# A two-layer encoder with mixture of experts: the residual in DRAM during the expert stage, with weighted expert rows added to it by indirect stores

## What is computed

```python
def hierarchical_moe(h, ...):
    ...
    weights = pg[:, None] * top_p                      # two experts for each token
    eid = g[:, None] * EXPERTS_PER_GROUP + top_i       # out of 32
    ...
    xs = x2[slot_tok].reshape(n_blocks, MOE_BLK, d)
    def expert_block(args):
        xb, e = args
        hid = jax.nn.silu(xb @ w_gate[e]) * (xb @ w_up[e])
        return hid @ w_down[e]
    ys = lax.map(expert_block, (xs, block_e)).reshape(cap, d)
    out = jnp.zeros_like(x2).at[slot_tok].add(ys * slot_w[:, None])

def reference(...):
    for i in range(DEPTH):
        hn = rmsnorm(x, norm_mix[i])
        x = x + (windowed_gqa_attention(hn, ...) if i % 2 == 0 else differential_attention(hn, ...))
        x = x + hierarchical_moe(rmsnorm(x, norm_ffn[i]), ...)
    return rmsnorm(x, final_norm)
```

## Time and profile before

| | |
|---|---|
| median of 3 runs | 2630.5 us (2630.07 to 2634.17) |
| the profiled execution | 2631.06 us |
| its span | 2629.4 us |
| mean granted clock of PE | 0.951 |
| busy PE / DVE / ACT / POOL | 2330.4 / 1869.7 / 1552.1 / 282.9 us |
| moved by DMA | 538.48 MB |

### The profile page before, as it was taken

The page is one execution under the profiler, slowest core; times in us unless marked ns, Lnnn a source line. Parts: engine busy times, 40 slices in busy tenths (PEclk is TensorE's granted clock), DMA queues, the critical chain, the costliest instruction groups (busy, mean ns, idle before and its releaser), DMA issues. The chain is left out here.

```text
span 2629.4 us, 34467 instructions
## 1 busy us (share of the span) xinstructions
PE 2330.4 (89%) x11464; PEld 1758.9 (67%) x11464; DVE 1869.7 (71%) x2461; ACT 1552.1 (59%) x2036; POOL 282.9 (11%) x260
## 2 busy tenths in 40 slices
PE   7899989569999999929999999998955999999991
PEld 6666658447777777727777777776844777777671
DVE  5775572668898888858556666556256888888895
ACT  5554460447777777735555565555043778777772
POOL 0000020012121111030000000002001122211102
PEclk9999999779999999959999999999977999999996
DMA  3012020469999999852000000002146999999995
GB/s 121 25 55 96 24 72 32 170 227 397 392 395 399 402 394 395 338 174 89 24 24 24 24 24 24 0 24 72 32 171 206 390 394 401 398 394 393 403 360 212
DMA packets 129501, 538.48 MB, mean 205 GB/s; under 512 B 23232, under 2 KB 52032, under 8 KB 80288
## 3 DMA queue, kind: packets, MB, share of 16 engines
q1 hardware_dynamic: 110496, 470.62, 47.1%
q0 software_dynamic: 18944, 67.12, 7.3%
HBM read 487.50 MB, written 50.20 MB: 204 GB/s over the span
## 5 line engine op out<-in xcount | busy, mean ns | idle before, releaser
L1507 DVE TENSOR_TENSOR m_lo_gate<-m_raw_gate,m_hi_gate 128x2048 fp32r<-128x2048 f32 x132 | 298.9, 2290 | 81.7 <-ACT m_hi_gate L1502 79.8
L1507 DVE TENSOR_TENSOR m_lo_up<-m_raw_up,m_hi_up 128x2048 fp32r<-128x2048 f32 x128 | 292.5, 2285 | 7.1 <-ACT m_hi_up L1502 7.0
L1507 DVE TENSOR_TENSOR m_lo_down<-m_raw_down,m_hi_down 128x2048 fp32r<-128x2048 f32 x124 | 280.2, 2283 | 13.7 <-ACT m_hi_down L1502 13.7
L1502 ACT CAST m_hi_down<-m_raw_down 128x2048 fp32r<-128x2048 f32 x124 | 236.2, 1907 | 90.7 <-DMA m_raw_down<-in_moe_w_down_dram 54.8
L1502 ACT CAST m_hi_gate<-m_raw_gate 128x2048 fp32r<-128x2048 f32 x132 | 247.8, 1908 | 25.6 <-DMA m_raw_gate<-in_moe_w_gate_dram 25.4
L1502 ACT CAST m_hi_up<-m_raw_up 128x2048 fp32r<-128x2048 f32 x128 | 244.4, 1911 | 22.2 <-DMA m_raw_up<-in_moe_w_up_dram 21.2
L1622 PE MATMUL m_G<-m_hi_gate,m_x_hi 128*96 128x512 f32 x512 | 206.1, 402 | 11.4 <-DVE m_x_lo L1732 11.3
L1622 PE MATMUL m_U<-m_hi_up,m_x_hi 128*96 128x512 f32 x512 | 205.2, 401 | 0.0
L1623 PE MATMUL m_G<-m_hi_gate,m_x_lo 128*96 128x512 f32 x512 | 204.6, 400 | 0.0
L1624 PE MATMUL m_G<-m_lo_gate,m_x_hi 128*96 128x512 f32 x512 | 202.5, 395 | 0.0
L1623 PE MATMUL m_U<-m_hi_up,m_x_lo 128*96 128x512 f32 x512 | 201.8, 394 | 0.0
(11 more groups left out here) (380 smaller groups left out, 4907.9 us busy)
## 6 DMA issues: line engine op xcount, KB each, us to landing
m_raw_gate<-in_moe_w_gate_dram SPq DMA_DIRECT2D x128, 1024.0 KB, 11.1
m_raw_up<-in_moe_w_up_dram SPq DMA_DIRECT2D x128, 1024.0 KB, 12.8
m_raw_down<-in_moe_w_down_dram SPq DMA_DIRECT2D x124, 1024.0 KB, 12.0
out_rows<-m_y POOLq DMA_DIRECT2D x64, 384.0 KB, 7.5
a1n_rows<-in_diff_w_qkv_dram SPq DMA_DIRECT2D x21, 512.0 KB, 5.5
out_rows<-a0n_gain SPq DMA_DIRECT2D x1, 8064.0 KB, 37.3
x_res<-in_x_dram SPq DMA_DIRECT2D x4, 1024.0 KB, 9.6
a0n_rows<-in_swa_w_o_dram SPq DMA_DIRECT2D x8, 512.0 KB, 3.3
```

The costliest lines, as they stand in the source:

```text
L1502: act.copy(self.hi[w][:, cut], self.raw[w][:, cut]).then_inc(self.hi_done[w], 1)
L1507: eng.tensor_tensor(self.lo[w][:, cut], self.raw[w][:, cut], self.hi[w][:, cut].bitcast(F32), ALU.subtract)\
```

## The change

x leaves SBUF after a route stage's norm has read it, and comes back with the expert outputs already added.

- In the route stage SP stores each tile of x to the DRAM tensor `x_rows` (1024 by 1024), right behind the store of the same tile's normed rows.
- The table gets as many columns again for the weights: the product on PE is 96 by 110, and `row_hot` is made by three operations of 16 by 55 elements. A slot that no token has gets the row number 2048 or above, and the weight 0 (`share`).
- In the expert stage ACT's copy of Y scales by the slot's share, and POOL's store is an indirect DMA that adds y into the rows of `x_rows` (`compute_op=ALU.add`). Gather and store carry a bound of 1023: rows beyond it are neither read nor written. POOL clears xg once before the first gather.
- `Combined` is gone, with `choice_slot`, `out_rows` and the zeros. Layer 1's attention norm and the final norm use `Loaded` with eight loads of one tile each, layer 0's too.
- Layer 1's attention stage no longer stores x. In the final norm the gain is loaded behind x.

The diff, cut:

```diff
 class Loaded(Resident):
...
-            sp.dma_start(self.t.x[:, 2 * i:2 * i + 2, :], self.x_rows[2 * i * P:2 * (i + 1) * P, :]
-                         .rearrange("(a p) n -> p a n", p=P)).then_inc(loaded, 16)
+            sp.dma_start(self.t.x[:, i, :], self.x_rows[i * P:(i + 1) * P, :]).then_inc(loaded, 16)
-class Combined:
...
# route
-                norm.sync_store(sp)
+                norm.sync_store(sp, lambda tt: sp.dma_start(moe.x_rows[tt * P:(tt + 1) * P, :], t.x[:, tt, :])
+                                .then_inc(x_stored, 16))
...
+                sp.wait_ge(x_stored, 16 * NT)
...
-                own(tt_(row_hot[:, :, :], over_slots(row[:, :], CAP),
-                        count_up[:, :].unsqueeze(1).broadcast_to((P, 2 * NT, CAP)), ALU.is_equal))
-                for c in range(TOP_K):
-                    half = row_hot[:, c * NT:(c + 1) * NT, 0:COLS]
-                    own(tt_(half, half, token[:, :].unsqueeze(2).broadcast_to((P, NT, COLS)), ALU.mult))
+                owned, shared = row_hot[:, :, 0:COLS], row_hot[:, :, COLS:2 * COLS]
+                own(tt_(owned, over_slots(row[:, :], COLS),
+                        count_up[:, 0:COLS].unsqueeze(1).broadcast_to((P, 2 * NT, COLS)), ALU.is_equal))
+                own(tt_(shared, owned, over_slots(weight[:, :, :].rearrange("p c a -> p (c a)"), COLS), ALU.mult))
+                own(tt_(owned, owned, over_slots(token[:, :], COLS), ALU.mult))
...
-                own(dve.tensor_copy(moe.table[:, :], L_ps[0:CAP, 0, 0:COLS]))
+                found = L_ps[0:CAP, 0, 0:COLS]
+                own(ts_(pad_row[:, :], found, 0.0, float(NOWHERE + 1), ALU.is_equal, ALU.mult))
+                own(dve.scalar_tensor_tensor(out=moe.table[:, :], in0=found, scalar=-1.0, in1=pad_row[:, :],
+                                             op0=ALU.add, op1=ALU.add))
+                own(dve.tensor_copy(moe.share[:, :], L_ps[0:CAP, 0, COLS:2 * COLS]))
# experts, POOL
                         pool.indirect_dma_start(out=xg[:, :], out_offset=None, in_=self.hn_rows,
-                                                in_offset=bass.IndirectOffsetOnAxis(pick[:, :], 0)).then_inc(gathered, 16)
+                                                in_offset=bass.IndirectOffsetOnAxis(pick[:, :], 0),
+                                                bounds_check=T - 1, oob_is_err=False).then_inc(gathered, 16)
 
                     def store(b):
+                        wait_count(pool, y_added, 16 * b)
+                        pool.tensor_copy(goal[:, :], self.table[:, b:b + 1] if isinstance(b, int) else self.table[:, bass.ds(b, 1)])\
+                            .then_inc(aimed, 1)
                         pool.wait_ge(y_copied, b + 1)
-                        rows = self.out_rows.rearrange("(r c) n -> r c n", c=CAP)
-                        pool.dma_start(rows[b] if isinstance(b, int) else rows[bass.ds(b, 1)].rearrange("r c n -> (r c) n"),
-                                       y[:, :]).then_inc(y_stored, 16)
-
+                        wait_apart(pool, aimed, b + 1, aim_seen)
+                        pool.indirect_dma_start(out=self.x_rows, out_offset=bass.IndirectOffsetOnAxis(goal[:, :], 0), in_=y[:, :],
+                                                in_offset=None, bounds_check=T - 1, oob_is_err=False,
+                                                compute_op=ALU.add).then_inc(y_added, 16)
+
+                    pool.memset(xg[:, :], 0.0).then_inc(cleared, 1)
+                    pool.wait_ge(cleared, 1)
# experts, ACT
-                        wait_count(act, y_stored, 16 * b)
-                        act.copy(y[:, :].rearrange("q (n m) -> q n m", n=2), Y[0:CAP, :, :]).then_inc(y_copied, 1)
+                        wait_count(act, y_added, 16 * b)
+                        share = self.share[:, b:b + 1] if isinstance(b, int) else self.share[:, bass.ds(b, 1)]
+                        act.activation(y[:, :].rearrange("q (n m) -> q n m", n=2), Y[0:CAP, :, :], ACT.Copy, scale=share)\
+                           .then_inc(y_copied, 1)
```

More of the change, by code:

```diff
@@ L132, in complete, with __init__ @@
         pass
-    def add(self, dve, tt):
-        pass
 class Loaded(Resident):
-    def __init__(self, t, x_rows):
+    def __init__(self, t, name, x_rows):
         self.t, self.x_rows = t, x_rows
-        self.loaded = [t.sem(f"x_loaded_{i}") for i in range(NT // 2)]
+        self.loaded = [t.sem(f"{name}_loaded_{i}") for i in range(NT)]
     def load(self, sp):
         for i, loaded in enumerate(self.loaded):
-            sp.dma_start(self.t.x[:, 2 * i:2 * i + 2, :], self.x_rows[2 * i * P:2 * (i + 1) * P, :]
-                         .rearrange("(a p) n -> p a n", p=P)).then_inc(loaded, 16)
+            sp.dma_start(self.t.x[:, i, :], self.x_rows[i * P:(i + 1) * P, :]).then_inc(loaded, 16)
     def complete(self, eng, tt):
-        eng.wait_ge(self.loaded[tt // 2], 16)
-class Combined:
[L157 to L173, removed]
-        for c in range(TOP_K):
[L175 to L184, removed]
+        eng.wait_ge(self.loaded[tt], 16)
 class Norm:
@@ L237, in sync_store @@
               .then_inc(self.rows_stored[tt % self.bufs], 16)
+            beside(tt)
     def sync_stored(self, sp):
@@ L465, in windowed_attention @@
         TB, O = TO[:, 0:2, :], TO[:, 2:4, :]
-        norm = Norm(t, "a0n", gain, sb, TO, Loaded(t, x_rows))
+        norm = Norm(t, "a0n", gain, sb, TO, Loaded(t, "a0x", x_rows))
         q_parts = sb("a0_q_parts", [P, QH, T], F32R)
@@ L844, in route @@
         stepped = v("stepped", 2 * NT * STEPS)
-        expert, row, slot_of_row = (v(what, 2 * NT) for what in ("expert", "row", "slot_of_row"))
+        expert, row = v("expert", 2 * NT), v("row", 2 * NT)
         owner_cmp, ctl_f = v("owner_cmp", (COLS - EXPERTS) * EXPERTS), v("ctl_f", COLS + 1)
@@ L979, in _ @@
                 own(dve.reciprocal(den[:, :], den[:, :]))
-                own(tt_(t.weight[:, 0, :], pg[:, :], den[:, :], ALU.mult))
-                own(tt_(t.weight[:, 1, :], t.weight[:, 0, :], ex[:, :], ALU.mult))
+                own(tt_(weight[:, 0, :], pg[:, :], den[:, :], ALU.mult))
+                own(tt_(weight[:, 1, :], weight[:, 0, :], ex[:, :], ALU.mult))
                 dve.wait_ge(counted, 1)
@@ L1066, in differential_attention @@
         probs = sb("a1_probs", [P, 2, 2, T], F32)
-        norm = Norm(t, "a1n", gain, sb, TO, Combined(t, "a1", t.dram[1], [probs[:, i // 2, i % 2, :] for i in range(4)]))
+        norm = Norm(t, "a1n", gain, sb, TO, Loaded(t, "a1x", x_rows))
         mix = sb("a1_mix", [P, 4, T], F32)
@@ L1105, in _ @@
                 norm.sync_load(sp)
+                norm.source.load(sp)
+                projections.load(sp, 0)
                 sp.dma_start(lam_b[:, :, :], lam.unsqueeze(0).broadcast_to((P, 4, HEAD))).then_inc(lam_loaded, 16)
                 sp.dma_start(sub_g[:, :], subln.unsqueeze(1), allow_slow_non_contiguous=True).then_inc(lam_loaded, 16)
-                norm.source.complete(sp, 1)
-                projections.load(sp, 0)
-                norm.source.complete(sp, NT - 1)
-                for tt in range(NT):
-                    sp.dma_start(x_rows[tt * P:(tt + 1) * P, :], t.x[:, tt, :]).then_inc(x_stored, 16)
                 projections.sync(sp, HEADS)
@@ L1119, in _ @@
             def _(pool):
-                norm.source.gather(pool)
                 pool.iota(bias[:, :].bitcast(I32), pattern=[[-1, SPAN]], base=T - P, channel_multiplier=1).then_inc(iota_done, 1)
@@ L1431, in _ @@
             def _(sp):
+                source.load(sp)
                 sp.dma_start(gain_b[:, :], gain.broadcast_to((P, D))).then_inc(gain_loaded, 16)
@@ L1437, in _ @@
                 sp.wait_ge(stored, 16 * NT)
-            @block.gpsimd
-            def _(pool):
-                source.gather(pool)
             @block.scalar
@@ L1609, in _ @@
                         store(b)
[L1611 removed]
+                    pool.wait_ge(y_added, 16 * (last + 1))
                 def times(pe, out, left, right, K, N, piece):
```

62 lines of the change are left out of this document (21 added, 41 removed).

## The result

The changed kernel takes 2653.28 us (median of 5 runs, 2647.22 to 2656.51) against 2630.5: 1.0084 times as long, 95% interval 1.0065 to 1.0102. A gain of 27 us was forecast, and a loss of 23 came, outside the stated range. The profiled execution has a span of 2651.5 us, 22.1 more than before.

What follows compares the result with a forecast made beforehand. Expert stages were taken as bound by PE early and DMA late, with PE waiting at the norms outside. Terms -19.0 - 13.8 - 5.2 + 5.0 + 4.0 + 2.0 gave -27.0, so 2604 us; range 2596 to 2650.

Steps and rivals of the forecast that it cites:

- What bounds the kernel: Expert stages: PE paces the first half at 17.64 us a block, DMA the rest, needing some 0.2 us more.
- (1): Layer 1's attention norm: without gathers and adds, 25.2 us to the first projection product, a gain of 19.0 us.
- (2): Final norm: without gathers and adds, 28.8 us instead of 42.6, a gain of 13.8 us.
- Term (3): Expert stages: dropped pads bring a block's DMA time to 17.5 us, so PE paces throughout, gaining 5.2 us.
- Term (4): Expert stages: waiting for y's store to land before the next copy costs 0, 14.0 us being under 17.64.
- Term (5): End of each expert stage: the last store stands alone before the barrier, +2.5 us, twice.
- (6): Route stage's tail: larger table and row_hot, small DVE operations and clearing xg, +2.0 us, twice.
- (7): Route stage's norm: eight more stores of x on SP's queue delay DVE, +1 us, twice.
- Rival C: Expert stages: adds hold the DMA engines, 18.6 us a block and up, slower at 2653 us; chance 0.09.
- pads that the bound does not drop: Expert stages, within Rival C: bounds check fails to drop pads, 18.8 us a block, 2664 us; no separate chance.

Runs made afterwards that it cites:

- e4: Changed kernel with pads added too, each to a spare row of its own in a longer x_rows, gather still dropping them: 2657.86 us, 1.0101 of before.
- e9: Like e5, but the k-th token goes to slot 12 (k mod 8) + k div 8: 2653.79 us, 1.0097 of before.
- e5: Changed kernel with slots dealt out: a block's k-th token goes to slot 6 (k mod 16) + k div 16: 2606.41 us, 0.9915 of before.
- e8: e5 with the final norm's gain loaded ahead of x: 2602.49 us, 0.9896 of before.
- e6: Edits of e4 and e5 together, slots dealt out and pads added, against the changed kernel: 2619.88 us, 0.9967 of before.

## Why the prediction was wrong

- **What bounds the kernel** was read rightly: PE's pace and DMA's lie 0.2 us apart, so the stage goes over to DMA at once when DMA's work grows.
- **Terms (1) and (2), the norms,** held: 25.0 us where 25.2 was forecast, 29.6 where 28.8 was, DVE waiting for the gain (8.97 us).
- **Term (3), the expert stages, failed.** It wrote "64 rows gathered 0.6; 64 rows added, 0.6 for the write and 0.6 more", the mean load of 16 engines, and came to 17.5 us a block where 18.67 was measured. The price of the add was nearly right: 0.6 for the write and 0.6 for the read is 1.2 us a block, the packets took 1.39 (88.8 / 64). By the Trainium skill (Collectives: The Full Stack, "The bandwidth ceiling: the fold count and why AG ≠ RS ≠ AR") the add of a ReduceScatter halves the rate because it reads two sources; the page writes that of a collective's ring, and 0.35 against 0.17 us a row agrees for this DMA. The rule, cited for 17.5 us a block, was right about the row and silent about the engines. What failed is "a third of every gather and store on average": with packed tokens the fullest engine keeps six rows of each (e4 adds 32 rows a block for 0.05 us, e9 and the packets show the groups of six). The fullest engine's sum is 3.30 us in place of before's 2.28, 1.0 more, and 18.67 in place of the late 17.85 is what came, 0.8 more.
- The Trainium skill (DMA: Bandwidth & Descriptors, "Why a DMA increments its semaphore by 16 and not by 1") says that some direct copies that POOL issues use all 16 engines with a sixteenth of the partitions each, rounded up; 96 partitions would give six each, an estimate from that rule. It says so of direct copies; e5 and e9 agree with it for the indirect ones. It was there to be read and was not put to the sum.
- **Term (4), y's round trip at 0,** held: at most 13.1 us to the landing, against a bound of 15.9. **Term (5)** was +2.5 twice, and came as +1.2 and +4.2, so 5.4 for 5.0. **Terms (6) and (7)** were +3.0 a layer; +2.4 and +1.1 came. A profiled execution is too coarse for that check: e5 and e8 have the same instructions up to the final norm, and their first copies of Y start at 590.2 and 585.5 us. The three operations took 1.08 us each, as forecast. PE's table product, priced at +0.8, was shorter than before:

```profile
525.05 1.08 DVE L980 TENSOR_TENSOR m0r_row_hot<-m0r_row,m0r_count_up 128x880 f32<-128x880 f32 x1
...
530.20 4.90 PE L882 MATMUL m0r_L<-m0r_row_hot,m0rn_hnT 128*96 128x110 f32 x32 [16.43 <-DVE m0rn_hnT L984]
```

- **Rival C** had the outcome to the microsecond (2653) with 0.09 of the chance. That is luck in the number: 18.6 us a block was where that rival began and no sum of anything, and its reason, the adds hold the engines, is the add's price, which was nearly right and in the forecast already. It stood beside the case of pads that the bound does not drop, at 2664; in effect that is what happened, with pads that are dropped and save nothing. The range ended 3 us below the result because most of C lay outside it.

What stays open: why the gather's rows weigh more on the interval than their packets' time. From e4 to e6 two rows less on the fullest engine are 0.4 us by the price and 0.8 measured. A gather's packets are spread over as long a time as an add's (3.84 and 3.75 us for 96 rows) though each is shorter (0.21 and 0.34 us); whether that is the reason was not tried. That a slot belongs to an engine in sixes is inferred from e5, e9, the sum and the packets in flight; no record names the engine of a packet.

## What to carry to other kernels

The indirect transfers here, spread over 16 engines, ended with their fullest engine, so price one by the rows of that engine, not by bytes over the total rate; dropped rows paid only when they were dealt over all engines. With the valid rows of an indirect DMA packed at the front, a bound that drops a third of the adds bought 4.6 us here, no more than the noise, with the rows dealt out 13.5, and the dealing alone turned a loss of 0.8% into a gain of 0.85%. An added row cost its DMA engine two plain ones (0.34 and 0.17 us), and that is worth paying where DMA has slack, or where it empties a stage border (32 us at the two norms).

## What was unexpected of the hardware

- DMA share is no measure of a DMA limit here: it is 1.00 in the DMA-paced window of e9 and 0.99 in the PE-paced one of e5, at 364 and 374 GB/s.
- POOL's issue of an indirect DMA depends on what runs beside it. The add's issue took 2.28 us in the middle in the changed kernel and 5.05 in e5, between ends of 1.4 and 5.3 in both; the tile's view of e5:

```profile
L1548 POOL DMA_INDIRECT x_rows<-m_y,m_goal x64: 1432/5052/5262, 592.3 to 2563.9; - x64
```

  In the prediction up to 5.5 us was worked out from what the Trainium skill states of the shared port pair (SBUF — State Buffer, "SBUF: two separate sides"). The rows agree in size; that the port is the cause wasn't tested.
- With the scaled copy of Y (1.11 us for 1.01) PE's pace was 17.67 to 17.70 us a block in place of 17.64, without a wait that names it; that the copy is the cause isn't shown.
